# Four column positions in turn for the near products of the gated recurrences

## The reference

```python
def chunked_gated_linear_attention(q, k, v, log_g):
    """o_t = S_t^T q_t,  S_t = diag(exp(log_g_t)) S_{t-1} + k_t v_t^T, chunkwise."""
    bc = jnp.cumsum(to_chunks(log_g), axis=3)
    def step(state, inp):
        q_, k_, v_, b_ = inp
        o_inter = jnp.einsum('bhik,bhkv->bhiv', q_ * jnp.exp(b_), state)
        rel = jnp.where(causal, b_[:, :, :, None, :] - b_[:, :, None, :, :], NEG)
        attn = jnp.einsum('bhik,bhjk,bhijk->bhij', q_, k_, jnp.exp(rel))
        o_intra = jnp.einsum('bhij,bhjv->bhiv', attn, v_)
        ...
```

## Time and profile before

| | |
|---|---|
| time, median of 3 runs | 2504.12 us (2502.79 to 2504.5) |
| span of the profiled execution | 2505.3 us |
| TensorE busy | 2471.3 us, 99% |
| VectorE, ScalarE, GpSimd busy | 678.3, 464.7, 135.5 us |
| stretch of the recurrences, first layer | about 832 to 1000 us |
| the same, second layer | about 1370 to 1536 us |

### The profile page before, as it was taken

One profiled execution on the slowest core, in us unless ns is written; L12 is line 12 of the kernel. 1 busy time (PEld: TensorE's weight loads), 2 busy tenths in 40 slices (PEclk: granted clock), 3 DMA queues, 4 the chain that ended last, 5 costly groups with the idle time before them and its releaser, 6 DMA issues.

```text
span 2505.3 us, 47503 instructions
## 1 busy us (share of the span) xinstructions
PE 2471.3 (99%) x21555; PEld 1466.0 (59%) x21555; DVE 678.3 (27%) x1393; ACT 464.7 (19%) x789; POOL 135.5 (5%) x333
## 2 busy tenths in 40 slices
PE   9999999999999999999999999999999999999999
PEld 8766557856555776888445885344443534353444
DVE  3534633434543443111014542001010101011012
ACT  1522321332323442000014441000000000000001
POOL 5011000011000310000001210000000000000000
PEclk9999999999999899999999999999999999999999
DMA  7522344431235412444436314999999999999992
GB/s 243 155 85 69 101 123 144 142 102 63 90 102 152 152 63 94 138 164 145 153 125 169 108 57 180 390 405 386 392 391 382 373 385 393 405 380 390 393 379 95
DMA packets 194431, 542.32 MB, mean 216 GB/s; under 512 B 29200, under 2 KB 61360, under 8 KB 194224
## 3 DMA queue, kind: packets, MB, share of 16 engines
q1 hardware_dynamic: 180576, 536.82, 58.6%
q10 hardware_dynamic: 13344, 1.35, 0.4%
q0 software_dynamic: 304, 1.05, 0.1%
HBM read 538.12 MB, written 1.05 MB: 215 GB/s over the span
## 4 chain that ended last, share of the span: by engine, by line
PE 96%; DVE 2%; ACT 1%; issue 1%; DMA 0%; ACTq 0%; DVEq 0%
PE psum L2726 23%; PE psum L407 18%; PE psum L2739 12%; PE psum L2341 8%; PE psum L710 7%; PE psum L1488 4%; PE psum L2362 4%; PE psum L1670 4%; PE psum L2227 2%; PE psum L472 1%; PE psum L2784 1%; PE psum L2777 1%; PE psum L1026 1%; PE psum L1030 1%; PE psum L1983 1%
## 5 line engine op out<-in xcount | busy, mean ns | idle before, releaser
L407 PE MATMUL psum<-ring,hT 128*128 128x512 f32 (+3 forms) x1120 | 469.8, 571 | 4.4 <-ACT area L829 2.7
L2726 PE MATMUL psum<-ring,mix 128*32 128x448 f32 x4608 | 438.7, 539 | 0.2 <-DVE mix L2988 0.2
L407 PEld LDWEIGHTS psum<-ring,hT 128*128 128x128 f32 x1120 | 207.1, 190 | 214.2 <-issue 190.5
L2726 PEld LDWEIGHTS psum<-ring,mix 128*32 128x32 f32 x4608 | 148.9, 110 | 282.6 <-issue 280.8
L2341 PE MATMUL psum<-hT,ring 128*128 128x256 f32 x896 | 193.7, 379 | 0.0
L2341 PEld LDWEIGHTS psum<-hT,ring 128*128 128x128 f32 x896 | 170.1, 190 | 23.0
L710 PE MATMUL psum<-hT,ring 128*128 128x256 f32 x768 | 166.4, 379 | 0.0
L710 PEld LDWEIGHTS psum<-hT,ring 128*128 128x128 f32 x768 | 145.9, 190 | 20.7 <-issue 1.0
L2739 PE MATMUL psum<-area 128*32 128x256 f32 x2688 | 148.2, 379 | 0.9 <-DVE area L2979 0.9
L2977 DVE TENSOR_TENSOR area<-area,psum 128x1344 f32<-128x1344 f32 x16 | 24.6, 1535 | 457.5 <-PE psum L2726 457.5
L2726 PE MATMUL psum<-area,mix 128*32 128x448 f32 x1536 | 147.2, 539 | 0.0
(11 more groups left out here) (530 smaller groups left out, 2419.0 us busy)
## 6 DMA issues: line engine op xcount, KB each, us to landing
ring<-in_w_in_dram SPq DMA_DIRECT2D x88, 1024.0 KB, 5.1
ring<-in_moe_w_gate_dram SPq DMA_DIRECT2D x96, 896.0 KB, 7.1
ring<-in_moe_w_up_dram SPq DMA_DIRECT2D x96, 896.0 KB, 7.7
area<-in_moe_w_down_dram SPq DMA_DIRECT2D x112, 512.0 KB, 5.9
ring<-in_moe_w_down_dram SPq DMA_DIRECT2D x112, 512.0 KB, 6.3
area<-in_moe_w_gate_dram SPq DMA_DIRECT2D x32, 896.0 KB, 7.5
area<-in_moe_w_up_dram SPq DMA_DIRECT2D x32, 896.0 KB, 7.0
ring<-in_w_out_dram SPq DMA_DIRECT2D x16, 1024.0 KB, 5.1
```

The costliest lines, as they stand in the source:

```text
L407: last = nc.tensor.matmul(acc(g)[:, t, 0:d["n"]], lhs(kk, t), w[:, k, :], start=kk == 0, stop=kk == d["nk"] - 1)
L2726: last = nc.tensor.matmul(PS[32 * j:32 * j + 32, 3 * p + b, 0:PIECE].rearrange("p (m n) -> p m n", n=32), tokens(k, b), w[:, :, j, :], sta ...
```

## The change

Inside `gla_pe`, and only there, the products of a unit are issued in another order and in other pieces:

- The near products go level by level, and in each level over the four blocks, so that the column position changes with every product: 6 levels x 4 blocks (now L2229). Then the two products of level 5 (L2231).
- The 64-key product is made as two of 32 keys by 64 queries (L2234), the 128-key product as four of 32 keys by 128 queries (L2238). Each writes the same numbers to the same place as before.

Products per unit: 27 before and 28 after for `t` = 0, 28 before and 32 after for `t` = 1. The semaphore `gla_prod` is counted up by the last of them as before; no other instruction changes.

```diff
-                for b in range(4):
-                    blk, c = slice(t * P + 32 * b, t * P + 32 * b + 32), slice(32 * b, 32 * b + 32)
-                    for l in range(5):
-                        nc.tensor.matmul(ps[c, 32 * l:32 * l + 32], GE[f][r, l, blk], GE[f][r, l, blk],
-                                         start=True, stop=True)
-                    nc.tensor.matmul(ps[c, 160:192], TT[r, FAM[f][1], blk], TT[r, FAM[f][0], blk], start=True, stop=True)
-                    if b % 2 == 0:
-                        up = slice(t * P + 32 * b + 32, t * P + 32 * b + 64)
-                        nc.tensor.matmul(ps[c, 192 + 32 * b:224 + 32 * b], GE[f][r, 5, blk], GE[f][r, 5, up], start=True, stop=True)
-                last = nc.tensor.matmul(ps[0:64, 224:288], GE[f][r, 6, t * P:t * P + 64],
-                                        GE[f][r, 6, t * P + 64:t * P + 128], start=True, stop=True)
+                blk = [slice(t * P + 32 * b, t * P + 32 * b + 32) for b in range(4)]
+                part = [slice(32 * b, 32 * b + 32) for b in range(4)]
+                for l in range(6):
+                    for b in range(4):
+                        k, q = (GE[f][r, l, blk[b]],) * 2 if l < 5 else (TT[r, FAM[f][1], blk[b]], TT[r, FAM[f][0], blk[b]])
+                        nc.tensor.matmul(ps[part[b], 32 * l:32 * l + 32], k, q, start=True, stop=True)
+                for b in (0, 2):
+                    nc.tensor.matmul(ps[part[b], 192 + 32 * b:224 + 32 * b], GE[f][r, 5, blk[b]], GE[f][r, 5, blk[b + 1]],
+                                     start=True, stop=True)
+                for b in range(2):
+                    last = nc.tensor.matmul(ps[part[b], 224:288], GE[f][r, 6, blk[b]], GE[f][r, 6, t * P + 64:t * P + 128],
+                                            start=True, stop=True)
                 if t == 1:
-                    last = nc.tensor.matmul(ps[:, 288:416], GE[f][r, 7, 0:P], GE[f][r, 7, P:S],
-                                            start=True, stop=True)
+                    for b in range(4):
+                        last = nc.tensor.matmul(ps[part[b], 288:416], GE[f][r, 7, 32 * b:32 * b + 32], GE[f][r, 7, P:S],
+                                                start=True, stop=True)
                 last.then_inc(sem("gla_prod"), 1)
```

## The result

The changed kernel takes 2489.14 us (median of 4 runs, 2486.39 to 2491.03), the kernel before 2503.45 (median of 4, 2502.14 to 2504.5): ratio 0.9945, interval 0.9931 to 0.9959. That is 14.3 us faster, where 24 were forecast. 2489 lies in the range of 2466 to 2494, but outside the forecast's own 2473 to 2487; the range reached that far for the rivals' sake, and the time alone would fit the slow feed (2491) better than the forecast (2480). The profile has to tell them apart.

A forecast was written before the change was run, and what follows sets the result against it. TensorE bounds the kernel, busy 99% of the span. 35.2 us saved in units, less 8.0 per layer to waits, leaves 19; plus 5 from the clock, 24 us off 2504.12: 2480 us, own range 2473 to 2487, full range 2466 to 2494.

The forecast's parts named there:

- the slow feed: Rival: TensorE's queue feeds records no closer than 17 ns, 0.4 us less saved per unit, 2491 us; chance 0.13.
- Cost of a unit: In gla_pe, four positions side by side: first-half unit 0.70 us for 1.71, second-half 0.92 for 2.12; 35.2 us in all.
- The rule of the Trainium skill: Loads of a unit, all on the same rows, would stand in line: 2502 us, as the shared-load-path rival; chance 0.05.
- What the waits take: TensorE's waits for other engines' chains take back 8.0 of 17.6 us saved per layer, leaving 19 in both.
- the named places: Waits at L1775 (1.8 us lost), L1973 and L2206 (1.0 each) and L472 (1.0): 4.8 us per layer.
- the quarter of the rest: A quarter of the other 12.8 us per layer, 3.2 us, lost at places with margin under 1 us, none shown.
- The clock: In the gla_pe stretches, denser units leave TensorE less time at half clock: 5 us more gained in two layers.
- I take half of the stretches as going: Half of the half-clock stretches in gla_pe's layers vanish: 5 us per layer, 2.5 to 3 after waits.
- The number: Whole kernel: 24 us saved, 2480 us, range 2466 to 2494; chance of the forecast's own range 0.58.
- The baseline: Profiled execution's span, 2505.3 us, taken as 1.2 over the median of three runs, 2504.12, from which the forecast is subtracted.

The follow-up runs named there:

- e6: Changed kernel with the 24 near products of each unit computed twice, in turn over the positions; 2498.1 us, ratio to the kernel before 0.9977.
- e1: Against the changed kernel, the 64- and 128-wide products left whole, near products still in turn; 2487.49 us, ratio to the kernel before 0.9944.
- e7: Kernel before the change with the 24 near products of each unit computed twice, in blocks; 2575.11 us, ratio 1.0274.
- e9: Changed kernel plus idle identity products in each layer, 12 before L1775's wait and 16 before L1796's; 2487.61 us, ratio to the kernel before 0.9929.
- e12: Changed kernel plus idle identity products sized to the waits, 7 before L1775's, 9 before L1796's, 4 at L1973; 2483.05 us, ratio to the kernel before 0.9917.

## Why the prediction was right, and where not

- *Cost of a unit.* Right. 0.70 us forecast and 0.68 measured for the first half; starts 9 ns apart (8.3 in e6) for 8 forecast; busy time 35.5 us less for 35.2. The second-half unit of GLA was undersized: 1.37 us saved for 1.2, because its pieces run beside the first products of `out`. In HGRN2, whose 64-row units the prediction did not look at, they don't, and the 1.2 is right. The rule of the Trainium skill ("TensorE: Matmul & The Clock Gate", Part 3, The mechanism) that a load overlaps only with another row group would have left the unit at 1.5 us or more. No run bears it out for column positions: all 52 small records of a GLA unit have the same 32 rows, and in e6 94 such records start within 0.81 us, 8.6 ns apart.
- *What the waits take.* Right in sum, 8.0 us per layer forecast, 9.0 measured (17.9 / 2). Of the named places L1775 came out at 1.9 for 1.8, L1973 at 2.2 in all for 1.0 on top of 1.2, L2206 at 2.1 in one layer, L472 at 1.1 for 1.0. The largest, 2.3 us at L1796, was not named; it fell under the quarter of the rest. But a fixed share of every saved microsecond is the wrong form. By e1 and the full change the waits take 7 of the first 25 us and all of the next 11: what is lost depends on how much has been saved already.
- *The clock.* Wrong. "I take half of the stretches as going" was 5 us; measured was none in the profile, and 2.7 us the other way in the runs. The step that fails is that a denser unit lets half of the slow stretches go: TensorE was at half clock for 48 us before and 48 after. In part the new waits stand against it: that at L1796 is followed by a fall in both layers (0.70), and filled it is not. I had named this ("where TensorE then waits the clock may fall as before") and still took the half. It is not the whole cause: behind the new wait at L1775 the clock is no worse than at the same place before, and what brings on the other falls of the changed kernel stays open.
- *The number.* That 2489 lies in the range owes something to the range's width: it was drawn for a slow feed, which e6 rules out. The feed was as fast as forecast; most of what is missing is the clock's.
- *The baseline.* I took the profiled execution, 2505.3 us of span, as 1.2 over the median. In the changed kernel a run is 1.8 longer than its span (2489.54 and 2487.7). By that the profiled run before was one of about 2507.1, 3.6 over the median of 2503.45. The profiles differ by 17.6 us and the medians by 14.3.

In one sum: 19 forecast for units and waits, 17.2 measured at equal clock; 5 forecast for the clock, -2.7 measured.

What stays open: which property of the work in one column position lowers the clock while TensorE is busy (the earlier trace rows show 0.50 with TensorE busy throughout, and e7 0.980 over the whole run), why a wait of 2 us is followed by a fall at L1796 and mostly not at L1775, and why the reordered plan costs 8 us with the old units and nothing with the new ones.

## What to carry to other kernels

Small fp32 products in 32-row tiles belong in turn over the four column positions: 30 ns a record became 8.3. Before paying for the last part of such a change, ask for TensorE's idle time after the first: here turning alone gave all that the neighbours let through, and the pieces another 11 us of shorter work that turned into waiting. Where runs of one kernel scatter with the granted clock, compare at equal clock before crediting an edit, and where a short wait can't be filled with real work, idle products that just fit into it can pay by the clock: 6 us here. And before a fall of the clock is put down to a wait, look at the same place in the other layer and in the kernel without the wait.

## What the runs showed of the hardware

- 94 matmul records of 32x32 fp32 over four column positions with the same rows started within 0.81 us, 8.6 ns apart, and 48 of them added 0.40 us to a unit (e6); in one position at a time they take 30 ns (e7).
- Products of two loops alternate where both use 32-row positions (1.00 us for the unit up to L2207), and not where one has 64 rows and the other 32 (1.14 us).
- Behind a pause of 2.35 us at L1796 the granted clock was 0.70 over the next 5.6 us, in both layers; with TensorE kept busy in it 1.00 (e9, e12). Behind pauses of 1.9 us at L1775 it was 0.68 once and 1.00 three times.
- The same 1536 added records left the mean clock at 0.9905 in turn, and took it from 0.992 to 0.980 in blocks, with TensorE 99% busy.
- A run's time follows its mean clock by 1.9 us for each 0.001. In full that would be 2.5 (0.001 of 2500 us). No run shows where the rest stays; part of a slow stretch may lie in time in which TensorE would have waited anyway.
